# Ten of twelve modulation vectors computed inside the attention stage of a two-layer diffusion backbone

## The chip, the cores and the metric

One core of a Trainium2 chip runs one launch of the kernel. The metric is device time in microseconds (us) of that launch. Engines: TensorE (PE), VectorE (DVE), ScalarE (ACT), GpSimd (POOL) and SyncE (SP, which only issues transfers). Everything is float32. Large products are made as three products of a high and a low float32r part; small ones (scores, transposes, values) as plain float32 products.

## The reference, cut to what matters

Two groups of tokens, 128 context and 512 latent ones of width 1024, go through two layers with shared weights. Each layer has six modulation vectors for each group, from the group's condition vector:

```python
mod_ctx = (jax.nn.silu(c_ctx) @ w_mod[l] + b_mod[l])[None, None, :]
mod_lat = (jax.nn.silu(c) @ w_mod[l] + b_mod[l])[:, None, :]
shift1, scale1, gate1, shift2, scale2, gate2 = jnp.split(mod, 6, axis=-1)
h = rms_norm(x, lp["g_norm1"]) * (1 + scale1) + shift1
mixed, ctx_t = token_mixing(h, lp, lam_init, ctx)     # four attention mixers, gates, w_out
x = x + gate1 * mixed
h = rms_norm(x, lp["g_norm2"]) * (1 + scale2) + shift2
x = x + gate2 * expert_choice_ffn(h, ...)             # 16 experts, each takes its top tokens
```

`w_mod` is 2 x 1024 x 6144 float32, 50 MB. One vector is a 1024-wide sixth of a layer's row, for both groups. The first product needs only shift1 and scale1 of layer 0; gate1 is needed after its attention, shift2, scale2 and gate2 after that, and the six of layer 1 later still.

## The kernel before, in words

**Modulation (front).** For each of 12 vectors q (`for q in range(L * 6)` on TensorE, ScalarE and VectorE), SyncE (L523) brings 8 chunks of 128x1024 of `w_mod` into a ring of 8 slots of 512 KB. ScalarE copies a chunk to its high part (`split_high`, L1023), VectorE subtracts for the low part (`split_low`, L1329), and TensorE (`mod_rows`, L640 to L643) multiplies with `csT`, the conditions in high and low parts. VectorE adds the bias (`mod_evac`, L1371), TensorE adds the high and low rows with `pair_sum` (`mod_tail`, L652), VectorE copies out, for the two scale vectors as (1 + s) times the norm's gain (`mod_copy`, L1385, L1387), and ScalarE stores to `mod_dram` (`mod_store`, L1048). While vector q is split, the first four chunks of vector q + 1 are too; behind the last vector these are the first four chunks of `w_in`.

**Rows from DRAM.** GpSimd loads each vector, broadcast over 128 partitions, as a scale-and-gain or shift tile (`mod_in`, L1787) just before the stage that uses it. The first ones are loaded once vectors 0 and 1 are stored, beside the rest of the front.

**Dense stretch.** Per layer, norm and transposes, then w_in in pieces (D, Aq, Akv), each of four chunks (two of the eight k rows each), tile after tile of 128 tokens (T = 5 tiles); the last tile frees the four chunks. The ring has 8 slots, the high parts 4. From the next piece on, `HIGH` = 4 chunks are split ahead, always when a chunk is freed.

**Attention.** 80 units (a head and a block of 128 queries) in the order D (units 0 to 19), A (20 to 39), B (40 to 59), C (60 to 79). In step ui TensorE makes `scores(ui)`, `turn(ui - 1)` (transposes of the probabilities) and `values(ui - 2)`, and in the three gaps after them (slots 0, 1, 2) what a table gives: chunks of the remaining dense pieces (`W` Bq, Bkv, C; gates `G`; branch outputs `B`), preparation of the next head (`prep`) and turns of o. The table is made by `plan_steps()`; `plan_uses()` gives every item one of two PSUM banks in turn, and an item that comes in while a tile of four chunks is open gets the other bank. All engines walk the same table. VectorE's order in a step is: in A the combination of two probability maps (L1504), the row maximum (L1583, L1588), slot 0, the copy of the fifth transposed block (L1596), slot 1, the scaling of o (L1608), slot 2. TensorE's `values` wait for that copy.

**GpSimd in attention** works in a fixed order: rotary tiles of A, the bias tables of B (`na_load`, L1843), four rotary tiles of C (`rope_c_tile`, L1774 to L1778), with a reload of a bias table that waits for a row maximum of step 46 after the first, then sums of gated outputs (L1889), and the tokens and gate1 for the residual.

**After attention:** the last gates, w_out (two pieces), residual, second norm, router, and 16 experts streamed through a ring of 16 slots that overlays the attention buffers.

## Time and profile before

| | |
|---|---|
| median of 3 runs | 2993.22 us (2990.93 to 2998.76) |
| profiled execution, its own time | 2989.55 us |
| its span, first to last instruction | 2987.6 us |
| granted TensorE clock, mean | 0.961 |
| TensorE, VectorE, ScalarE, GpSimd busy | 90%, 67%, 53%, 15% |
| front: start to the last evacuation of a vector | about 184 us |
| dense stretch of layer 0 | 206 to 285 us |
| attention steps of layer 0 | 285 to 804 us |
| experts of layer 0, of layer 1 | about 1000 to 1540, 2400 to 2940 us |

The profiled execution is one run, 3.7 us below the median. Busy time of a matmul is modelled and overlaps the next; idle time of an engine counts only where another waits for what it does next.

### The profile page before, as it was taken

How to read it: one execution, taken by the hardware profiler on the slowest of the kernel's cores; microseconds unless marked ns; L12 is line 12 of the kernel's file. 1: busy time of each engine (PE TensorE's matmuls, PEld its weight loads, DVE VectorE, ACT ScalarE, POOL GpSimd, SP SyncE). 2: the span in 40 equal slices, each digit the busy share in tenths (PEclk: the TensorE clock that was granted, in tenths of full speed). 3: DMA queues.
4: the chain of work that ended last, by engine and by line, in shares of the span. 5: the costliest groups of instructions: out<-in, count | busy, mean ns of one | idle time of the engine just before them, and what ended most of it. 6: DMA issues, size and time to landing. Idle time of an engine off the chain costs nothing.

```text
span 2987.6 us, 40730 instructions
## 1 busy us (share of the span) xinstructions
PE 2686.8 (90%) x13616; PEld 1916.9 (64%) x13616; DVE 1987.8 (67%) x3069; ACT 1575.4 (53%) x2278; POOL 462.2 (15%) x335
## 2 busy tenths in 40 slices
PE   6779999999996699999988999999999499999994
PEld 1248777777775466666657777777777366666662
DVE  7864356535336799999975346643434699999994
ACT  5643344334323577777753444433422387777773
POOL 0003000212130112112211200031122112211201
PEclk8989999999998899999998999999999699999997
DMA  9942012112144699999983211121134399999994
GB/s 333 333 144 89 29 37 60 50 44 63 67 157 148 231 375 380 381 377 378 381 283 107 73 33 36 36 71 43 43 113 153 113 361 380 382 376 382 381 382 145
DMA packets 190521, 593.80 MB, mean 199 GB/s; under 512 B 22945, under 2 KB 32991, under 8 KB 190391
## 3 DMA queue, kind: packets, MB, share of 16 engines
q1 hardware_dynamic: 171638, 527.66, 48.0%
q0 software_dynamic: 18640, 64.20, 7.4%
q8 instruction: 79, 1.29, 0.2%
q14 instruction: 52, 0.42, 0.0%
q10 hardware_dynamic: 112, 0.23, 0.0%
HBM read 566.78 MB, written 25.23 MB: 198 GB/s over the span
## 4 chain that ended last, share of the span: by engine, by line
PE 77%; DVE 10%; issue 5%; ACT 5%; DMA 2%; ACTq 0%; SPq 0%; POOL 0%; DVEq 0%; POOLq 0%
PE bank L466 21%; PE bank L468 20%; PE bank L467 20%; PE bank L837 4%; PE bank L809 4%; DVE low L1329 2%; ACT high L1023 2%; PE bank L827 2%; PE bank L641 1%; PE bank L640 1%; DMA ring<-in_w_mod 1%; DVE st L1583 1%; PE bank L949 1%; PE bank L981 1%; DVE sigr L1513 1%
## 5 line engine op out<-in xcount | busy, mean ns | idle before, releaser
L1023 ACT ACTIVATE high<-ring 128x1024 fp32r<-128x1024 f32 (+1 forms) x1008 | 1053.8, 1052 | 447.0 <-PE bank L468 369.1
L1736 DVE TENSOR_TENSOR low<-ring,high 128x1024 fp32r<-128x1024 f32 x736 | 880.4, 1220 | 72.7 <-ACT high L1023 70.9
L466 PE MATMUL bank<-high,hT_high 128*128 128x512 f32 (+2 forms) x1280 | 520.9, 407 | 25.2 <-ACT sigr L1109 13.6
L467 PE MATMUL bank<-low,hT_high 128*128 128x512 f32 (+2 forms) x1280 | 485.4, 379 | 0.0
L468 PE MATMUL bank<-high,hT_low 128*128 128x512 f32 (+2 forms) x1280 | 484.2, 378 | 0.0
L1329 DVE TENSOR_TENSOR low<-ring,high 128x1024 fp32r<-128x1024 f32 (+2 forms) x272 | 321.8, 1210 | 138.7 <-ACT high L1023 137.7
L466 PE MATMUL bank<-high,xeT_high 128*80 128x512 f32 x1024 | 406.1, 397 | 2.1 <-DVE xeT_low L1334 2.1
L468 PE MATMUL bank<-high,xeT_low 128*80 128x512 f32 x1024 | 403.9, 394 | 0.0
L467 PE MATMUL bank<-low,xeT_high 128*80 128x512 f32 x1024 | 403.6, 394 | 0.0
L1210 ACT ACTIVATE att<-bank,st 128x640 f32<-128x640 f32 (+3 forms) x200 | 136.7, 684 | 351.2 <-DVE st L1588 256.5
L466 PEld LDWEIGHTS bank<-high,hT_high 128*128 128x128 f32 x1280 | 243.7, 190 | 78.4 <-ACT sigr L1109 18.2
L468 PEld LDWEIGHTS bank<-high,hT_low 128*128 128x128 f32 x1280 | 242.7, 190 | 47.4
L467 PEld LDWEIGHTS bank<-low,hT_high 128*128 128x128 f32 x1280 | 244.3, 191 | 32.5
L1583 DVE TENSOR_REDUCE st<-bank 128x1 f32<-128x640 f32 (+3 forms) x200 | 136.6, 683 | 116.6 <-PE bank L809 114.4
L466 PE MATMUL bank<-high,hidT_high 128*80 128x512 f32 x512 | 203.9, 398 | 10.6 <-DVE hidT_low L1334 8.9
L468 PEld LDWEIGHTS bank<-high,xeT_low 128*80 128x80 f32 x1024 | 151.8, 148 | 84.7 <-issue 0.7
L466 PEld LDWEIGHTS bank<-high,xeT_high 128*80 128x80 f32 x1024 | 151.9, 148 | 83.4 <-DVE xeT_low L1334 2.6
L467 PEld LDWEIGHTS bank<-low,xeT_high 128*80 128x80 f32 x1024 | 152.3, 149 | 80.4 <-issue 0.7
L468 PE MATMUL bank<-high,hidT_low 128*80 128x512 f32 x512 | 202.8, 396 | 0.0
L467 PE MATMUL bank<-low,hidT_high 128*80 128x512 f32 x512 | 202.7, 396 | 0.0
L1923 POOL DMA_INDIRECT x_resid<-oTr,idx_s x32 | 91.5, 2860 | 686.2 <-DVE oTr L1699 667.2
L1914 POOL DMA_INDIRECT U<-x_normed,idx_g x32 | 132.1, 4129 | 327.3 <-issue 104.2
(237 smaller groups left out, 3298.6 us busy)
## 6 DMA issues: line engine op xcount, KB each, us to landing
ring<-in_w_e_gate SPq DMA_DIRECT2D x256, 512.0 KB, 6.2
ring<-in_w_e_up SPq DMA_DIRECT2D x256, 512.0 KB, 6.9
ring<-in_w_e_down SPq DMA_DIRECT2D x256, 512.0 KB, 6.4
ring<-in_w_mod SPq DMA_DIRECT2D x96, 512.0 KB, 6.0
ring<-in_w_gate SPq DMA_DIRECT2D x64, 512.0 KB, 3.9
ring<-in_w_in SPq DMA_DIRECT2D x24, 512.0 KB, 4.5
ring<-in_w_branch SPq DMA_DIRECT2D x16, 512.0 KB, 4.2
ring<-in_w_out SPq DMA_DIRECT2D x16, 512.0 KB, 4.8
```

The lines of the kernel that those rows point to most:

```text
L466: nc.tensor.matmul(out, lhs[0], rhs_high, start=start, stop=False)
L467: nc.tensor.matmul(out, lhs[0], rhs_low, start=False, stop=False)
L468: return nc.tensor.matmul(out, lhs[1], rhs_high, start=False, stop=stop)
L809: ins = mm(ps[p % 2][:, col:col + w], qT[r0:r0 + rn, b, un["m"] * P:(un["m"] + 1) * P], kT[r0:r0 + rn, b, a:a + w], start=True, stop=True)
L837: ins = mm(bank(6, P, P + HD), probT[:, ui % 2, i * P:(i + 1) * P], v_src(un, kb), start=(i == 0), stop=(i == len(un["kb"]) - 1))
L1023: A(high[:, HSLOT[g], :, 0:w], ring[:, SLOT[g], :, 0:w], ACT.Copy).then_inc(high_done, 1)
L1210: A(prob[:, p % 4, 0:w], ps[p % 2][:, 0:w], ACT.Exp, bias=negm[:, p % 8:p % 8 + 1], scale=SCALE[un["br"]], accum_out=sm[:, p % 8:p % 8 + 1 ...
L1329: V.tensor_tensor(low[:, SLOT[g], :, 0:w], ring[:, SLOT[g], :, 0:w], high[:, HSLOT[g], :, 0:w].bitcast(F32), ALU.subtract).then_inc(low_dv ...
L1583: then(V.tensor_reduce(mx[:, c8:c8 + 1], S[:, 0:w], AX.X, ALU.max))
L1736: V.tensor_tensor(low[:, SLOT[ahead], :, :], ring[:, SLOT[ahead], :, :], high[:, HSLOT[ahead], :, :].bitcast(F32), ALU.subtract).then_inc( ...
L1914: pool.indirect_dma_start(out=xe[0:CAP, b, :], out_offset=None, in_=xn_dram, in_offset=bass.IndirectOffsetOnAxis(ap=idx_g[:, b, 0:1], axis ...
L1923: pool.indirect_dma_start(out=x_dram, out_offset=bass.IndirectOffsetOnAxis(ap=idx_s[:, e, 0:1], axis=0), in_=ybuf[0:CAP, e, :], in_offset= ...
```

## The change

Vectors 0 and 1 of layer 0 (shift1, scale1) are still made in the front. The other ten are made in attention: six (gate1, shift2, scale2, gate2 of layer 0, shift1 and scale1 of layer 1) in the attention of layer 0, four (the rest of layer 1) in that of layer 1. A vector is cut into four sums of 256 columns, 24 sums in layer 0 and 16 in layer 1. A sum is made from four pieces; a piece is one transfer of 256 KB (two of the eight k rows, 256 columns) into one of two slots. VectorE multiplies each row by the condition's column of k, for both groups, and accumulates into a tile of 128 x 512 (four instructions of 128x256 a piece). TensorE then adds the 128 partitions by a plain float32 product with a column of ones (128x1), ScalarE copies the 1x512 result to row 0 of the tile, and GpSimd stores it to `raw_dram`. For each four sums GpSimd loads the vector back as 128x16, adds the bias, makes (1 + s) g for the scale vectors, and stores to `mod_dram`. Sum i is added in step 8 + 68 i // 24, slot 1; its pieces stand in the three steps before, in slots 0, 2, 1 and 0. The ring of the dense stages has 6 slots instead of 8; slots 6 and 7 hold the pieces (6) and the accumulators (7).

```diff
 RING_E = 16
 HIGH_E = 8
+RING_D = 6
-N_MOD = 6 * D // NW
-CH_MOD = NQ * N_MOD * L
+CH_MOD = 2 * KD
...
+MOD_COLS = 256
+MOD_ROWS = 2
+VECTORS = [[(0, 2), (0, 3), (0, 4), (0, 5), (1, 0), (1, 1)], [(1, 2), (1, 3), (1, 4), (1, 5)]]
+SUMS = [[(lv, v, a) for lv, v in vs for a in range(D // MOD_COLS)] for vs in VECTORS]
+N_PIECE = KD // MOD_ROWS
+def sum_step(i):
+    return 8 + 68 * i // len(SUMS[0])
...
+    for i in range(len(SUMS[0])):
+        for k in range(N_PIECE):
+            at[sum_step(i) - 3 + 2 * k // 3][2 * k % 3].append(("piece", i, k))
+        at[sum_step(i)][1].append(("sum", i))
...
-        a, h = (SLOT_E[e % RING_E], e % HIGH_E) if e >= 0 else (g % RING, g % HIGH)
+        a, h = (SLOT_E[e % RING_E], e % HIGH_E) if e >= 0 else (g % RING if g < CH_MOD else (g - CH_MOD) % CH_LAYER % RING_D, g % HIGH)
...
+                def mod_fills(step):                      # SyncE
+                    while mods and mods[0][0] < step:
+                        nn = mods.pop(0)[1]
+                        i, k = divmod(nn, N_PIECE)
...
+                        if nn >= 2:
+                            sp.wait_ge(mod_used, MOD_ROWS * (nn - 1))
...
+                        sp.dma_start(mod_w[:, nn % 2, :, :], src).then_inc(mod_w_in[nn % 2], 16)
...
-            for q in range(L * 6):                        # TensorE
+            for q in range(2):
                 mod_rows(q)
                 if q:
                     mod_tail(q - 1)
...
+                def add_partitions(i):
+                    if i < len(SUMS[l]):
+                        n, r = SUM0[l] + i, USE["sum", i]
+                        bank_free(r)
+                        pe.wait_ge(mod_used, KD * (n + 1))
+                        mm(bank_use(r)[0:1, :], ones, mod_acc[:, n % 2, :], start=True, stop=True).then_inc(sum_full, 1)
...
+                def sum_out(i):                           # ScalarE
...
+                        act.wait_ge(sum_full, n + 1)
+                        A(mod_acc[0:1, n % 2, :], bank_use(USE["sum", i])[0:1, :], ACT.Copy).then_inc(sum_ev, 1)
...
+                def mod_piece(i, kp):                     # VectorE
...
+                    dve.wait_ge(mod_w_in[n % 2], 16 * (n // 2 + 1))
+                    if kp == 0 and i >= 2:
+                        dve.wait_ge(raw_out, 16 * (i - 1))
+                    for k in range(MOD_ROWS):
+                        if n or k:
+                            dve.wait_ge(mod_used, MOD_ROWS * n + k)
+                        for g in range(2):
+                            w, cc = mod_w[:, n % 2, k, :], csf[:, MOD_ROWS * kp + k, g:g + 1]
+                            dst = mod_acc[:, i % 2, g * MOD_COLS:(g + 1) * MOD_COLS]
+                            if kp == 0 and k == 0:
+                                ins = V.tensor_scalar(dst, w, cc, None, ALU.mult)
+                            else:
+                                ins = V.scalar_tensor_tensor(out=dst, in0=w, scalar=cc, in1=dst, op0=ALU.mult, op1=ALU.add)
+                        ins.then_inc(mod_used, 1)
...
+            def raw_store(i):                             # GpSimd
+                pool.wait_ge(sum_ev, i + 1)
+                if i:
+                    pool.wait_ge(raw_out, 16 * i)
+                pool.dma_start(raw_dram[...], mod_acc[0:1, i % 2, :]...).then_inc(raw_out, 16)
...
+                mod_work = []
+                for i in range(len(SUMS[l])):
+                    n = SUM0[l] + i
+                    mod_work.append((sum_step(i) + 1.5, raw_store, (n,)))
+                    if i % N_PIECE == N_PIECE - 1:
+                        mod_work.append((sum_step(i) + 2.5, fin_load, (VEC0[l] + i // N_PIECE, n)))
+                        mod_work.append((sum_step(i) + 3.5, fin_store, (VEC0[l] + i // N_PIECE,)))
...
-                rope_c_tile(0)
-                na_reload(0)
-                rope_c_tile(1)
-                rope_c_tile(2)
-                rope_c_tile(3)
+                for m in range(TS):
+                    mod_until(STEP_OF["dense", ("W", "C"), m, NQ - 1])
+                    rope_c_tile(m)
+                    if m == 0:
+                        na_reload(0)
```

`mod_until(step)` makes GpSimd do the parts of `mod_work` that are due before that step; it stands in front of each of its tasks in attention. `fin_load` issues four small loads (six for a scale vector), `fin_store` two or four small GpSimd operations and two stores. GpSimd waits for the vectors before it loads gate1, the rows of the second norm, and those of the next layer.

## Rows read from the trace of the kernel before

**Rows 1.** The page: busy shares; then TensorE, DMA and GB/s in 40 slices.
```profile
PE 2686.8 (90%) x13616; PEld 1916.9 (64%) x13616; DVE 1987.8 (67%) x3069; ACT 1575.4 (53%) x2278; POOL 462.2 (15%) x335
...
PE   6779999999996699999988999999999499999994
...
DMA  9942012112144699999983211121134399999994
```

**Rows 2.** Busy time by stretch: A:B length, PE, PEld, DVE, ACT, POOL, clock, DMA, GB/s.
```profile
50.00:100.00 50.00, 39.32 (x129) 10.17 (x130) 43.38 (x44) 30.78 (x31) 2.09 (x4) 0.90 0.95 349
...
302.00:391.00 89.00, 83.33 (x518) 67.26 (x516) 30.27 (x87) 36.73 (x81) 0.00 (x0) 1.00 0.12 37
391.00:527.00 136.00, 128.37 (x787) 102.70 (x788) 85.30 (x219) 61.02 (x132) 1.12 (x2) 0.99 0.15 45
527.00:660.00 133.00, 125.75 (x710) 101.16 (x709) 67.12 (x151) 47.39 (x89) 28.89 (x27) 1.00 0.16 48
660.00:785.00 125.00, 116.29 (x633) 91.48 (x632) 54.85 (x144) 51.50 (x118) 16.50 (x10) 1.00 0.18 56
```

**Rows 3.** Timeline of SyncE's queue (start, duration): w_mod's first 16 transfers; first small load.
```profile
4.36 25.38 SPq L523 DMA_DIRECT2D ring<-in_w_mod  x16
...
165.01 0.43 SPq L543 DMA_DIRECT2D qn_b<-in_mla_q_norm  x1
```

**Rows 4.** Timeline of VectorE: the last vector's evacuation; the first scaled row of the norm.
```profile
183.59 1.27 DVE L1371 TENSOR_TENSOR U<-bank,U 4x512 f32<-4x512 f32 x2
...
193.21 1.28 DVE L1418 SCALAR_TENSOR_TENSOR att<-att,st,M 128x1024 f32<-128x1024 f32 x1
```

**Rows 5.** Timelines: stores of vector 1 and the last two; broadcast loads; their landing.
```profile
61.14 0.24 ACTq L1048 DMA_DIRECT2D mod_rows<-U  x1
...
186.08 3.97 ACTq L1048 DMA_DIRECT2D mod_rows<-U  x2
...
66.29 0.53 POOL L1787 DMA_DIRECT2D M<-mod_rows  x1 [56.08 <-DMA mod_rows<-U]
...
L1787 POOL DMA_DIRECT2D M<-mod_rows x12: 528/536/601, 66.3 to 2264.3; - x12
...
DMA to landing us min/median/max: 5.0/6.4/10.7
```

**Rows 6.** Timeline of TensorE: two plain float32 products of 512 columns, four records.
```profile
137.25 1.87 PE L652 MATMUL bank<-U,pair_sum 4*2 4x512 f32 x4
```

**Rows 7.** TensorE's waits from 284 to 900: us in total, times, longest.
```profile
PE bank L466 <- ACT sigr L1109: 7.4, 8, 1.4
```

**Rows 8.** VectorE's group of 128x256 (busy, mean ns); two in the timeline.
```profile
L1460 DVE SCALAR_TENSOR_TENSOR sigr<-sigr,st,qn_b 128x256 f32<-128x256 f32 x10 | 4.8, 479 | 0.1
...
236.69 0.48 DVE L1460 SCALAR_TENSOR_TENSOR sigr<-sigr,st,qn_b 128x256 f32<-128x256 f32 x1
237.09 0.34 DVE L1462 SCALAR_TENSOR_TENSOR sigr<-sigr,st,M 128x128 f32<-128x128 f32 x1
```

**Rows 9.** Timelines in a step of D: VectorE's copy; TensorE's values.
```profile
357.02 0.29 DVE L1596 COPY att<-bank 128x128 f32<-128x128 f32 x1
...
357.41 1.30 PE L837 MATMUL bank<-M,att 128*128 128x64 f32 x10 [0.43 <-issue]
```

**Rows 10.** Timeline of GpSimd: reload, rope tiles 1 and 3; landing of L1816's small stores.
```profile
570.77 1.61 POOL L1843 DMA_DIRECT2D att<-rpb_padded  x2 [8.29 <-DVE st L1588]
572.40 1.28 POOL L1774 TENSOR_TENSOR U<-U,rope 128x192 f32<-128x192 f32 x2
...
581.20 2.14 POOL L1774 TENSOR_TENSOR U<-U,rope 128x192 f32<-128x192 f32 x2
...
L1816 POOL DMA_DIRECT2D out<-U x12: 545/565/600, 278.0 to 1972.9; - x12
...
DMA to landing us min/median/max: 1.8/2.5/4.6
```

**Rows 11.** DMA issues by line: transfers of 256 KB, median us to landing.
```profile
ring<-in_w_in SPq DMA_DIRECT2D x16, 256.0 KB, 3.2
```

More of the change, by code:

```diff
@@ L171, in plan_uses @@
     for x in order:
-        if x[0] == "on":
+        if x[0] in ("on", "piece"):
             continue
@@ L184, in plan_uses @@
             open_at = None
+        if x[0] == "sum":
+            freed[r] = ("sum", x[1])
+            continue
         by = "dve" if x[0] == "oT" or (x[0] == "dense" and x[1][0] == "B") else "act"
@@ L205, with mod_step_of @@
 USE, USE_BANK, BEFORE, FREED, FULL, N_USE, LOWS_AFTER, LOWS_END = plan_uses()
+STEP_OF = {x: i for i, step in enumerate(AT) for slot in step for x in slot}
+RELEASE_STEP = [-1] * RING_D + [STEP_OF.get(("dense", pc, T - 1, kq), -1 if pc[0] == "W" else 2 * N_UNIT)
+                                for pc in STREAM for kq in range(CHUNKS_IN[pc])] + [2 * N_UNIT] * (2 * NQ)
+def mod_step_of(n):
+    i, k = divmod(n, N_PIECE)
+    return sum_step(i) - 3 + 2 * k / 3
 def count_of(*key):
@@ L362, in hybrid_step @@
         csf = sb("csf", [P, KD, 2])
+        fin = sb("fin", [P, 3, 16])
+        mod_w = ring[:, RING_D, :, :].rearrange("p h (k n) -> p h k n", k=MOD_ROWS)
+        mod_acc = ring[:, RING_D + 1, :, :]
         csT = sb("csT", [P, KD, 4], F32R)
@@ L375, in hybrid_step @@
         lam, neglam = st[:, 148:150], st[:, 150:151]
+        ones = st[:, 158:159]
         lg = sb("lg", [P, T, NE])
@@ L398, in hybrid_step @@
         g_row_in = sem("g_row_in")
+        ones_set = sem("ones_set")
+        mod_w_in, mod_used = [sem(f"mod_w_in{i}") for i in range(2)], sem("mod_used")
+        sum_full, sum_ev, raw_out = sem("sum_full"), sem("sum_ev"), sem("raw_out")
+        fin_in, fin_out = sem("fin_in"), sem("fin_out")
         eps_set, sq_done = sem("eps_set"), sem("sq_done")
@@ L585, in matrix @@
                             sp.wait_ge(o_ev, N_UNIT * (l + 1))
+                        if i is None and SLOT[g + k] == RING_D:
+                            sp.wait_ge(raw_out, 16 * SUM0[l + 1])
                         if i is None and SLOT[g + k] == 13:
@@ L682, in bank_free @@
                 def bank_free(r):
-                    if BEFORE[r] is not None:
-                        by, n = FREED[BEFORE[r]]
-                        if by == "act":
+                    r = BEFORE[r]
+                    while r is not None and FREED[r][0] == "sum" and FREED[r][1] >= len(SUMS[l]):
+                        r = BEFORE[r]
+                    if r is not None:
+                        by, n = FREED[r]
+                        if by == "sum":
+                            pe.wait_ge(sum_ev, SUM0[l] + n + 1)
+                        elif by == "act":
                             pe.wait_ge(tile_act, N_USE["act"] * l + n)
@@ L857, in between @@
                             dense(*x)
+                        elif what == "sum":
+                            add_partitions(*x)
                         elif what == "prep":
@@ L1053, in _ @@
                 split_high(g)
[L1054 to L1065 removed]
+            bias_in(1)
+            for g in range(HIGH, CH_MOD + HIGH):
+                split_high(g)
+            for q in range(2):
                 mod_store(q)
@@ L1193, in between @@
                             prep_out(*x)
+                        elif what == "sum":
+                            sum_out(*x)
                         elif what == "oT":
                             turn_o_high(*x)
-                        elif x[0] == 2:
+                        elif what == "on" and x[0] == 2:
                             act.wait_ge(on_var, l + 1)
@@ L1357, in _ @@
             V.memset(eps, EPS).then_inc(eps_set, 1)
+            V.memset(ones, 1.0).then_inc(ones_set, 1)
             dve.sem_inc(hid_ready, BUF)
@@ L1391, in _ @@
                 split_low(g)
-            for q in range(L * 6):
+            for q in range(2):
                 for k in range(KD):
@@ L1551, in between @@
                                 split_low(chunk_no(l, c))
+                        elif what == "piece":
+                            mod_piece(*x)
                         elif what == "oT":
@@ L1804, in _ @@
                         mod_in(q1, g)
-                    for b in range(2):
-                        pool.wait_ge(mod_out[b], 16 * 3 * L)
                 def rope_rows(X, t0, tmp, heads, d4):
```

78 lines of the change are left out of this document (62 added, 16 removed).

## The prediction

> **What bounds the kernel now.** I read the page's busy shares and its 40 slices first, then the busy time by stretch, then each engine's timeline and the waits inside a stretch. TensorE is busy 90% of 2987.6 us, VectorE 67%; in the slices two long stretches have TensorE at 9 and DMA at 9 (the experts), and the first slices are different: DMA 9, TensorE 6 to 7 [rows 1]. This is the modulation, bound by streaming 50 MB of w_mod through ring, high/low split and matmul; VectorE is busy 43.4 of 50 us there, TensorE 39.3 [rows 2]. In attention the balance is reversed: TensorE is busy 83.3 of 89, 128.4 of 136, 125.8 of 133 and 116.3 of 125 us in the stretches of mixers D, A, B and C, VectorE 30.3, 85.3, 67.1 and 54.9, and DMA has a share of 0.12 to 0.18 [rows 2]. So DMA has room for anything in attention, VectorE has some, TensorE none: what is added to TensorE counts, and what is added to VectorE counts wherever TensorE waits for it.
>
> **What goes at the front.** SyncE issues its last w_mod transfer at 165.0 (the first small load follows at 165.01), and 18.6 us later, at 183.59, VectorE evacuates the last vector [rows 3, 4]. With two vectors only, the sixteenth w_mod transfer ends its issue at 29.74 [rows 3]; the same 17 small loads and the same four w_in chunks stand between it and the evacuation, so this comes at about 29.8 + 18.6 = 48.4. The shift is 135.2 us, or 13.5 for each of ten vectors.
>
> Part of it is given back. The rows of vectors 0 and 1 must now go through DRAM in the open. Before, the store of vector 1 was issued at 61.14 and GpSimd started the broadcast loads at 66.29, 5.15 later, with nobody waiting; two loads take 2 x 0.53 to issue and 5.0 to 6.4 to land [rows 5]: 11.2 to 12.6 from the store. Before, the last store was issued at 190.05 and the first scaled row started at 193.21 [rows 4, 5], so 8.0 to 9.4 are exposed. The w_in chunks will have landed by then, and GpSimd's small stores land in 1.8 at best and 2.5 in the middle (last line of [rows 10]) rather than 5; against that the slowest of these loads took 10.7. I take 7.5, ends 4 and 12. Net gain of the front: **128**.
>
> **What TensorE gets.** 24 + 16 = 40 products of ones (128x1) with 128x512 plain f32. The nearest row is the product with pair_sum, also f32 and 512 columns: four records in 1.87 us are two products, one record every 0.43, so 0.86 for one [rows 6]. 40 x 0.86 = 34. Some of it will lie under a wait for VectorE in the same step; I take three quarters, 26, ends 15 and 36. ScalarE's 40 copies of 1x512 hide, since it is busy under half of the time in attention [rows 2]; were TensorE not the bound, they would cost some 0.6 each.
>
> A sum also takes one of the two dense banks, and if a tile of four chunks is open in the other, the next tile gets the bank that was just closed and must wait for ScalarE to empty it. That wait exists in attention today behind the preps and the turns of o: 7.4 us in 8 cases [rows 7]. Half of 40 sums at 0.9, a third of them uncovered: 5, ends 0 and 18.
>
> **What VectorE gets.** Each sum has 4 pieces of 4 instructions of 128x256: 160 pieces, 640 instructions. The nearest row is a scalar_tensor_tensor 128x256 of 0.479 us; the next instruction starts 0.40 after it when it doesn't wait [rows 8]. The pair (0.40 + 0.48) is followed by a wait on its own semaphore, some 0.04, so a piece occupies 1.77 and all of them 283 us: 22, 28, 29 and 17 pieces in D, A, B and C of layer 0, 22, 28 and 14 in layer 1. Bounds: fully hidden 0; fully exposed 283.
>
> What is exposed is decided by where a piece stands. In D, VectorE has time, but its copy of the fifth block of transposed probabilities is tied to TensorE: copy at 357.02, done at 357.31, TensorE's values start at 357.41, after an idle of 0.43 [rows 9]. A piece in the first slot of such a step stands between the row maximum and this copy, and TensorE waits for nearly all of it; a piece in the second or third slot falls into an idle of 1 to 2.5 us. About a third of the pieces are of the first kind, at some 1.2: 0.41 each on average, 44 pieces, 18. In A, VectorE's 85 us plus 28 x 1.77 = 50 is 135 of 136 + 6 us: nearly full, in order, and unevenly loaded (splits and gate products come in groups); I take 0.54 for each of 56, 30. In B 0.35 for 43, 15, since the copy there has more slack; in C 0.24 for 17, 4. Together 67, a quarter of 283; for the range 25 and 120. VectorE's fill pushes nothing else that TensorE doesn't already stand for: dense lows are split four chunks ahead.
>
> The Trainium skill (VectorE: DVE Perf Modes, The TRN2 errata) prices a VectorE operation between SBUF tiles at 58 cycles plus one per element: 327 ns for 256 f32 elements, an estimate from that table. The row says 479, and the measurement decides. With 327 the 640 instructions would be 97 us shorter and the sum, at the same exposed quarter, lower by about 25.
>
> **The waits that are new.** VectorE's first piece of sum i waits for the DRAM store of sum i-2, which stands in GpSimd's order. GpSimd runs one rope tile of C, then waits for the maximum of step 46 (its reload starts at 570.77), and ropes tiles 1 and 2 before it comes to the store of sum 13, ahead of tile 3, which starts at 581.20 [rows 10]. VectorE needs that store in the first slot of step 47, one step of 133 / 20 = 6.65 us after that maximum, near 577. With a landing of 2.5 it waits about 7, and behind it stand its maxima and copies. TensorE has some 3 us of other work: 4 per layer, **8**, ends 0 and 16. The weight pieces themselves have two ring slots: 256 KB land in 3.2 us [rows 11], against a lead of 1.3 steps (8 us); only where two sums lie two steps apart is it close, and that is in the 67. SyncE issues them in the order of release, so a late piece holds back only the dense fill behind it. GpSimd's queue gets 40 stores, 46 loads and 20 stores more, at 0.53 each 56 us; it is busy 1.1 of 136 us in A and 28.9 of 133 in B [rows 2], so they hide, except at the place just told.
>
> **The ring shrinks from 8 slots to 6 in the dense stretches.** At D to Aq, Aq to Akv and inside w_out, chunks 3 and 4 of the next piece are fetched only when the last tile before it lets go of its chunks. 3.2 to 4.5 us of landing plus two splits of about 1.1 against four to five chunk times of 0.7 to 1.3: about 1 per border, three per layer, **6**, ends 0 and 20. The expert prefetch starts a little later but has the router's idle stretch to fill 16 slots: nothing.
>
> **Sum:** -128 + 26 + 5 + 67 + 8 + 6 = -16. The profiled execution took 2989.6, so 2974 by its measure; the median of the runs shown is 3.7 above it, hence 2977.
>
> **Rivals.**
> First, attention is elastic: idle time of VectorE in neighbouring steps takes up the pieces, 25 instead of 67 and no wait for stores: -128 + 34 + 25 + 8 = -61, about 2932; anything up to 2955 belongs here. For it: VectorE is at 34 to 63% by stretch [rows 2]. Against: the copy that is already tied to TensorE. Chance 0.24.
>
> Second, on the slow side: a VectorE piece in front of maximum, combine or copy is served in order, and TensorE waits for each. It decides once more than about 0.30 of the 283 us is exposed. At 0.40 it is 113: -128 + 30 + 113 + 19 = +34, about 3027. For it: A would be 95% full and D's copy has 0.1 us of slack. Against: the pieces are spread so that one or two fall in a step of 5 to 7 us. Chance 0.26.
>
> Third, GpSimd's order: its two rope products take 1.28 us in one tile and 2.14 in the next but one [rows 10], and all 38 waits for a store hang on it. At one microsecond each it is 30 more than my 8: about 3007. The Trainium skill (SBUF — State Buffer, SBUF: two separate sides) says that GpSimd and a VectorE operation with two SBUF inputs take a shared port pair in turns, the loser blocked for a whole instruction; the 1.28 and 2.14 would agree with it. Chance 0.07.
>
> Fourth, the change doesn't shorten the front as said, since the tokens or small loads land late when they follow closely: gain 100, about 3005. The tokens were asked for before 10 us, and nothing else is new. Chance 0.05.
>
> My forecast case (2955 to 2995) has 0.38. A measurement of this kernel can tell about 0.3%, 9 us, from no change: faster is below 2984, slower above 3002. The first rival and most of the forecast case give faster 0.51; its upper end and the mild forms of the others give same 0.17; slower 0.32. Range 2938 to 3025.
>
> **What would show it.** Right: first w_in product some 128 us earlier, near 78; about 40 products from mod_acc at 0.86; D, A, B, C of layer 0 longer by about 12, 22, 26 and 8, of layer 1 by as much except C, which stays; experts unchanged. TensorE idle in front of its values, and a VectorE wait of about 7 us on raw_out in step 47 of each layer. Wrong: attention longer by less than 60 (first rival) or by more than 140 (second), or VectorE waits on stores or on mod_w all over. A price of a piece below 1.5 or above 2 would spoil the largest term.

## The result and the profile after

The changed kernel takes **3066.53 us** (median of 4 runs, 3061.86 to 3068.37); the kernel before took 2994.67 in the same comparison (2990.93 to 2998.76). The ratio is 1.0237, 95% interval 1.0218 to 1.0257: slower by 72 us, where I had forecast 16 less and a range that ended at 3025. The profiled execution (its own time, 3068.37, is the highest of the four) has a span of 3066.6 us, 79.0 above that of before.

The front did what was forecast. These are timelines of the kernel after, SyncE's queue first, then VectorE, GpSimd and VectorE again (start, duration, engine, line, operation, output<-inputs, count, idle before and what ended it):

```profile
4.18 26.15 SPq L564 DMA_DIRECT2D ring<-in_w_mod  x16
30.36 0.43 SPq L584 DMA_DIRECT2D qn_b<-in_mla_q_norm  x1
...
48.88 1.27 DVE L1450 TENSOR_TENSOR U<-bank,U 4x512 f32<-4x512 f32 x2
...
57.01 0.53 POOL L1926 DMA_DIRECT2D M<-mod_rows  x1 [46.01 <-DMA mod_rows<-U]
...
62.79 1.28 DVE L1498 SCALAR_TENSOR_TENSOR att<-att,st,M 128x1024 f32<-128x1024 f32 x1 [4.32 <-DMA oTr<-mod_rows]
```

The last evacuation comes at 48.88 instead of 183.59, the first scaled row at 62.79 instead of 193.21 [rows 4]: 130.4 us earlier. So 209 us are lost behind that. To see where, I cut attention at the same instructions in both kernels: VectorE's scaling of o of units 0, 18, 38, 58 and 78, so that the four rows are nearly the mixers D, A, B and C of layer 0. Busy time by stretch (A:B length, PE, PEld, DVE, ACT, POOL, granted clock, DMA share, GB/s), before:

```profile
297.30:391.20 93.90, 87.80 (x551) 71.26 (x551) 32.07 (x93) 38.58 (x85) 0.00 (x0) 1.00 0.11 35
391.20:527.30 136.10, 128.47 (x788) 102.75 (x787) 85.40 (x219) 60.82 (x131) 1.12 (x2) 0.99 0.15 45
527.30:680.50 153.20, 142.98 (x801) 114.75 (x800) 73.05 (x163) 56.18 (x106) 30.05 (x28) 1.00 0.18 56
680.50:798.40 117.90, 111.16 (x601) 87.59 (x600) 59.20 (x150) 45.46 (x107) 23.57 (x15) 1.00 0.16 50
sum 501.10, PE 470.40 PEld 376.36 DVE 249.72 ACT 201.04 POOL 54.74; mean PE 117.60 PEld 94.09 DVE 62.43 ACT 50.26 POOL 13.69
```

and after:

```profile
169.10:279.70 110.60, 98.01 (x573) 74.93 (x572) 68.89 (x186) 42.22 (x90) 6.01 (x12) 0.97 0.27 87
279.70:451.60 171.90, 149.75 (x793) 109.95 (x791) 129.69 (x330) 64.49 (x137) 13.94 (x27) 0.91 0.26 76
451.60:643.20 191.60, 162.62 (x809) 123.05 (x810) 123.21 (x279) 60.10 (x113) 35.02 (x42) 0.92 0.28 85
643.20:781.30 138.10, 123.86 (x611) 91.78 (x610) 87.77 (x213) 48.22 (x112) 35.11 (x39) 0.94 0.23 70
sum 612.20, PE 534.24 PEld 399.70 DVE 409.56 ACT 215.03 POOL 90.08; mean PE 133.56 PEld 99.93 DVE 102.39 ACT 53.76 POOL 22.52
```

Layer 0's attention is 111 us longer: 16.7, 35.8, 38.4 and 20.2 by mixer. The same cut in layer 1, which has 16 sums instead of 24, gives 16.6, 34.6, 28.5 and 1.7 (C has no sum there), 81 in all. Outside attention 17 us more are lost: 2 before the first unit, 7 between attention of layer 0 and of layer 1, 8 behind that of layer 1. 111 + 81 + 17 - 130 = 79, the whole difference of the spans. Attention costs 193 us for 40 sums, 4.8 each, where the prediction's terms for it were 26 + 5 + 67 + 8 = 106.

In these rows VectorE is far from full (409.56 of 612 us) and has 160 us more to do, and two things happen to TensorE. Its idle time, length less busy, goes from 30.7 to 78.0 us. And its busy time grows by 64 us although the 24 products with ones account for some 25: the granted clock falls from 0.99 or 1.00 to between 0.91 and 0.97 while the number of other products stays. One minus the clock, times the length, summed over the four stretches is 42 us after against 1 before; this is an estimate of what the lower clock took. TensorE stalls, and in the same stretches it is also slower in between.

TensorE's and VectorE's waits from 160 to 790 us (engine line waited for: us in total, times, longest) show how short the stalls are:

```profile
PE bank L904 <- issue: 19.7, 11, 5.4
PE bank L507 <- ACT sigr L1178: 11.5, 8, 2.6
PE bank L904 <- ACT att L1301: 9.1, 6, 4.2
PE bank L894 <- DVE att L1584: 4.0, 5, 1.4
...
DVE ring L1612 <- issue: 8.1, 2, 7.0
DVE ring L1614 <- DMA ring<-in_w_mod: 3.2, 2, 2.2
```

L904 is the values, whose input VectorE copies at L1699. The largest of these waits are put down to "issue"; VectorE's timeline in mixer D says what was late:

```profile
194.22 0.82 DVE L1686 TENSOR_REDUCE st<-bank 128x1 f32<-128x640 f32 x1
195.08 0.15 DVE L1691 TENSOR_SCALAR st<-st 128x1 f32<-128x1 f32 x1
195.16 1.80 DVE L1614 SCALAR_TENSOR_TENSOR ring<-ring,csf 128x256 f32<-128x256 f32 x4
197.43 0.62 DVE L1612 TENSOR_SCALAR ring<-ring,csf 128x256 f32<-128x256 f32 x2 [0.47 <-DMA ring<-in_w_mod]
198.08 0.88 DVE L1614 SCALAR_TENSOR_TENSOR ring<-ring,csf 128x256 f32<-128x256 f32 x2
198.88 0.28 DVE L1699 COPY att<-bank 128x128 f32<-128x128 f32 x1
```

and TensorE's, of the same kernel:

```profile
195.06 0.40 PE L509 MATMUL bank<-high,hT_low 128*128 128x512 f32 x1
199.26 2.37 PE L904 MATMUL bank<-M,att 128*128 128x64 f32 x10 [3.81 <-issue]
```

Between the maximum and the copy stand not one piece but two, the last of one sum and the first of the next, with half a microsecond for weights on top; TensorE starts its values 0.10 us after the copy ends, idle for 3.81. In the kernel before, VectorE and TensorE in the same step (the one whose scaling of o is that of unit 5) had

```profile
320.77 0.29 DVE L1596 COPY att<-bank 128x128 f32<-128x128 f32 x1
321.56 1.22 PE L837 MATMUL bank<-M,att 128*128 128x64 f32 x10
```

so the copy was done 0.50 us before TensorE came to its values, which then had no idle time ahead of them. This is one of the worst places: two pieces meet in a slot four times in layer 0 and three times in layer 1, wherever two sums lie two steps apart. Elsewhere a first slot has at most one piece.

VectorE's copies in the four stretches of layer 0, first before, then after (the last numbers: busy, mean ns, idle before), show how its slack went:

```profile
L1596 DVE COPY att<-bank 128x128 f32<-128x128 f32 x46 | 13.4, 290 | 24.8 <-PE bank L827 24.2
L1699 DVE COPY att<-bank 128x128 f32<-128x128 f32 x46 | 13.2, 287 | 6.6 <-PE bank L894 6.1
```

Before, VectorE stood ready ahead of its copies for 24.8 us in all; after, for 6.6, and TensorE's idle time ahead of its values rose from 7.8 to 28.8 us. The copy itself is no slower, nor are the maxima of 640 columns (821 and 820 ns): VectorE's work comes later, it does not take longer.

### The profile page after: what moved, and what is told of

Read it like the earlier page. It is cut to its first block, busy times and chain, and to the rows that moved or that the text cites. A ratio compares the mean times of both kernels' runs of the same rounds, so it can differ in the third digit from the quotient of the medians.

```text
span 3066.6 us, 40985 instructions
## 1 busy us (share of the span) xinstructions
PE 2685.6 (88%) x13336; PEld 1929.1 (63%) x13336; DVE 2135.2 (70%) x3590; ACT 1519.2 (50%) x2238; POOL 500.0 (16%) x457
## 4 chain that ended last, share of the span: by engine, by line
PE 71%; DVE 11%; issue 8%; ACT 5%; DMA 4%; POOL 1%; SPq 0%; ACTq 0%; DVEq 0%; POOLq 0%
PE bank L507 19%; PE bank L509 18%; PE bank L508 18%; PE bank L904 4%; PE bank L876 3%; DVE low L1407 2%; ACT high L1100 2%; PE bank L894 2%; DVE ring L1614 1%; DVE st L1686 1%; PE bank L927 1%; DMA ring<-in_w_in 1%; PE bank L682 1%; PE bank L1058 1%; PE bank L1026 1%
## 5 line engine op out<-in xcount | busy, mean ns | idle before, releaser
L1100 ACT ACTIVATE high<-ring 128x1024 fp32r<-128x1024 f32 (+1 forms) x928 | 973.8, 1052 | 437.1 <-PE bank L509 380.1
L507 PE MATMUL bank<-high,hT_high 128*128 128x512 f32 (+2 forms) x1280 | 529.8, 414 | 43.1 <-ACT sigr L1178 20.3
L508 PE MATMUL bank<-low,hT_high 128*128 128x512 f32 (+2 forms) x1280 | 492.6, 385 | 0.0
L509 PE MATMUL bank<-high,hT_low 128*128 128x512 f32 (+2 forms) x1280 | 491.6, 384 | 0.0
L1288 ACT ACTIVATE att<-bank,st 128x640 f32<-128x640 f32 (+3 forms) x200 | 136.4, 682 | 435.2 <-DVE st L1691 329.9
L1407 DVE TENSOR_TENSOR low<-ring,high 128x1024 fp32r<-128x1024 f32 (+2 forms) x192 | 227.3, 1198 | 129.7 <-ACT high L1100 128.9
L507 PEld LDWEIGHTS bank<-high,hT_high 128*128 128x128 f32 x1280 | 248.0, 194 | 101.1 <-ACT sigr L1178 24.8
L1614 DVE SCALAR_TENSOR_TENSOR ring<-ring,csf 128x256 f32<-128x256 f32 x560 | 254.4, 496 | 9.9 <-DMA ring<-in_w_mod 4.0
```

The source lines that it names most:

```text
L507: nc.tensor.matmul(out, lhs[0], rhs_high, start=start, stop=False)
L508: nc.tensor.matmul(out, lhs[0], rhs_low, start=False, stop=False)
L509: return nc.tensor.matmul(out, lhs[1], rhs_high, start=False, stop=stop)
L1100: A(high[:, HSLOT[g], :, 0:w], ring[:, SLOT[g], :, 0:w], ACT.Copy).then_inc(high_done, 1)
L1288: A(prob[:, p % 4, 0:w], ps[p % 2][:, 0:w], ACT.Exp, bias=negm[:, p % 8:p % 8 + 1], scale=SCALE[un["br"]], accum_out=sm[:, p % 8:p % 8 + 1 ...
L1407: V.tensor_tensor(low[:, SLOT[g], :, 0:w], ring[:, SLOT[g], :, 0:w], high[:, HSLOT[g], :, 0:w].bitcast(F32), ALU.subtract).then_inc(low_dv ...
```

## The experiments

Times are compared by their ratio to the kernel before, timed beside them on the same chip; differences in us are these ratios' differences times 2995. The 95% intervals make a difference of two such ratios good to some 7 to 11 us.

**The ring alone.** The kernel before, with the ring in the dense stretches cut from 8 slots to 6.

```
-  a, h = (SLOT_E[e % RING_E], e % HIGH_E) if e >= 0 else (g % RING, g % HIGH)
+  a, h = (SLOT_E[e % RING_E], e % HIGH_E) if e >= 0 else (g % RING if g < CH_MOD else (g - CH_MOD) % CH_LAYER % RING_D, g % HIGH)
```

> The kernel before with 6 instead of 8 ring slots in the dense stretches, nothing else. My forecast had 6 us for it. In the changed kernel the stretches around attention (first scaled row to first unit, last unit to the experts) are longer by about 9 us per layer. If the ring is the cause of these: 12 to 20 us more than before. If something else there is (vectors read back late, clock): under 6.

Measured: 3008.24 us, ratio 1.0045 (1.0028 to 1.0062), 15 us above the 2993.19 of before, where the prediction had 6. The four stretches of attention kept their lengths (94.1, 136.4, 153.2 and 118.0 in layer 0); the loss is outside, 4 us before the first unit, 6 between the layers' attentions and 5 behind the second. That is most of the 17 us that the kernel after loses there.

**The parts one by one.** The kernel before with 6 slots, and of the change only VectorE's 640 instructions (on data that stay in memory; the first line below), only the 40 products and their copies (the second line), or both. No weights are loaded for them in any of the three, their results are not used, and the front still makes all twelve vectors; slots 6 and 7 are filled once per layer.

```
+  at[sum_step(i) - 3 + 2 * k // 3][2 * k % 3].append(("piece", i, k))
...
+  at[sum_step(i)][1].append(("sum", i))
```

> The kernel before with 6 slots and with VectorE's 640 instructions at the places of the change, on resident data: no w_mod transfer, no product, no store; all twelve vectors still made in the front. Theory A (VectorE serves pieces in order in front of what TensorE waits for; more than half of their 283 us is exposed): 120 to 170 us above the kernel with 6 slots alone, with the granted clock in attention down to 0.9 to 0.95. Theory B (the pieces are mostly hidden, as forecast, and the loss comes from stores, transfers and banks): under 70 above it.

> The kernel before with 6 slots and with the 40 plain products of 128x1 by 128x512 and ScalarE's copies at their places, on resident data; no VectorE work but one clearing per layer. 34 us for the products at 0.86 each, and up to 18 for the order of the two banks: 30 to 50 above the kernel with 6 slots alone. If the bank order were the large term that was missed: 80 or more.

> VectorE's pieces and the products together on resident data, with 6 slots: the change without its transfers, without GpSimd's stores and loads, without the shorter front. Theory A: about 170 to 190 above the kernel with 6 slots alone, so that stores and transfers are left with under 25 of the change's cost. Theory B: under 110. If the two parts hid one another: clearly less than the sum of their single costs.

Measured: 3155.34 (ratio 1.0536, 1.0509 to 1.0563), 3058.03 (1.0211, 1.0191 to 1.0232) and 3183.42 (1.0630, 1.0603 to 1.0657). Above the 3008.24 of the ring alone these are **147**, **50** and **175** us. VectorE's group in the first (layer 0's attention; busy, mean ns, idle before), and TensorE's in the second (48 records, two for each of 24 products):

```profile
L1554 DVE SCALAR_TENSOR_TENSOR ring<-ring,csf 128x256 f32<-128x256 f32 x336 | 155.5, 504 | 3.4
```

```profile
L885 PE MATMUL bank<-ring,ident 128*1 128x512 f32 x48 | 24.5, 591 | 3.3 <-ACT sigr L1144 1.4 <-DVE sigr L1562 1.1 <-ACT U L1136 0.7
```

The price of VectorE's instructions was right (a piece is busy for 1.80 where I had 1.77), and no weight, store or work of GpSimd was added with it: 147 of 283 us, 52%, are exposed with nothing added but this work in VectorE's order. TensorE's clock goes down with it: 0.97, 0.91, 0.92 and 0.95 in the four stretches of layer 0 with VectorE's work alone, against 0.98, 0.99, 1.00 and 1.00 with the products alone. With the products alone TensorE's idle time hardly changes (31.2 us in layer 0's attention for 30.9 with the ring alone). Together the two parts cost 22 less than one by one, as if some of the idle time that VectorE makes covered products. Front -130, ring 15 and both parts 175 make 60; the kernel after shows 72, and the rest, 12, is about the size of what these three kernels leave out, the waits for stores and weights; the waits at step 47, told below, make 10 of it.

**One instruction for four.** The kernel after, but a piece is one 128x512 instruction instead of four of 128x256. The same bytes are loaded, the same places are taken, and the sums are not those of the vectors.

```
-  for k in range(MOD_ROWS):
-      for g in range(2):
-          w, cc = mod_w[:, n % 2, k, :], csf[:, MOD_ROWS * kp + k, g:g + 1]
...
+  for k in range(1):
+      for g in range(1):
+          w, cc = mod_w[:, n % 2, :, :].rearrange("p k n -> p (k n)"), csf[:, MOD_ROWS * kp + k, g:g + 1]
...
```

> The changed kernel with one VectorE instruction of 128x512 a piece in place of four of 128x256 (the sums are then not the vectors' sums; all transfers, waits, products and stores stay). A piece takes about 0.75 instead of 1.8 us. Theory A: the cost of attention falls by 60% of VectorE's part, by 75 to 110 us, so 2955 to 2990. Theory B: stays above 3040.

Measured: 2978.09 us, ratio 0.9935 (0.9915 to 0.9955), 90 us below the kernel after and 19 below that of before. VectorE's groups in layer 0's attention:

```profile
L1614 DVE SCALAR_TENSOR_TENSOR ring<-ring,csf 128x512 f32<-128x512 f32 x72 | 56.5, 785 | 5.6 <-DMA ring<-in_w_mod 4.7 <-issue 0.9
...
L1612 DVE TENSOR_SCALAR ring<-ring,csf 128x512 f32<-128x512 f32 x24 | 11.6, 485 | 11.2 <-DMA mod_raw<-ring 8.2 <-DMA ring<-in_w_mod 2.0 <-issue 0.4
```

The pieces take 68 us here, against 170 in the kernel after. With 60% of VectorE's time gone, 60% of 147, 88, was to be expected if the exposed share is the same for short pieces as for long ones; 90 came back. So the loss goes mostly by VectorE's time, not by the number of places, loads or stores, which are unchanged. TensorE's clock is at 0.95 to 1.00 in the four stretches.

**The place.** No piece in the first slot of a step, that is none between the step's maximum and its copy:

```
+ PIECE_AT = [(-3, 2), (-2, 2), (-1, 1), (-1, 2)]
...
-  at[sum_step(i) - 3 + 2 * k // 3][2 * k % 3].append(("piece", i, k))
+  at[sum_step(i) + PIECE_AT[k][0]][PIECE_AT[k][1]].append(("piece", i, k))
```

> The changed kernel with the pieces in slots 2, 2, 1, 2 of the steps -3, -2, -1, -1 instead of 0, 2, 1, 0: none between the row maximum and the copy of the fifth block. If slot 0 is what costs, as I weighed it in D: 25 to 50 us less than the changed kernel. If any place costs alike, since combination and maximum are delayed instead: within 15 us of it.

Measured: 3057.93, ratio 1.0201 (1.0181 to 1.0221): 11 us better than the kernel after. In D, whose first slot the prediction had named, 5 us are won (105.4 instead of 110.6), in A 3, in B 6 are lost. TensorE's idle time in layer 0 moved rather than went: ahead of the values it fell from 28.8 to 16.2 us, ahead of the dense products it rose from 24.3 to 27.6 and ahead of the sums' products from 4.3 to 13.4. The first slot was not what mattered most; a piece in a later slot is in somebody's way too.

**The grain.** One row of two instructions in each slot in turn instead of a piece of two rows, so that no two rows meet in a slot:

```
+          ROW_AT.append(max(3 * sum_step(_i) - 9 + _k, ROW_AT[-1] + 1 if ROW_AT else 0))
...
-  for k in range(N_PIECE):
-      at[sum_step(i) - 3 + 2 * k // 3][2 * k % 3].append(("piece", i, k))
+  for k in range(KD):
+      at[ROW_AT[KD * i + k] // 3][ROW_AT[KD * i + k] % 3].append(("piece", i, k // MOD_ROWS, k % MOD_ROWS))
```

> The changed kernel with each piece cut in two, one row (two instructions, 0.9 us) in each slot in turn. Same VectorE time, same products. If single delays of 1.8 us exceed a slack of about one microsecond in each slot: 40 to 80 us less. If VectorE's total time is the bound: within 15 us.

Measured: 3033.4, ratio 1.0119 (1.0099 to 1.0139), 35 us better than the kernel after, between the two expectations. So about a quarter of VectorE's 147 us hung on how its work was spread. The version changes two things at once, the size of a lump and the share of the work in first slots (from half to a third), so the 35 are not the lumps' alone; the rest stays with one row to a slot.

**No VectorE at all.** TensorE makes the sums from the weights as they land, in plain f32: eight products of 128x2 with 128x256 in the place of one.

```
-  mm(bank_use(r)[0:1, :], ones, mod_acc[:, n % 2, :], start=True, stop=True).then_inc(sum_full, 1)
...
+  for k in range(KD):
+      ins = mm(bank_use(r, 0, MOD_COLS)[0:2, :], csf[:, k, :], mod_w[:, k // MOD_ROWS, k % MOD_ROWS, :],
+               start=(k == 0), stop=(k == KD - 1))
```

> A version meant to beat both: no VectorE work at all. The four pieces of a sum land in slots 6 and 7, and TensorE multiplies them itself in plain float32, the condition's columns (128x2, both groups) by 128x256, eight products a sum of some 0.21 us each, 1.7 a sum, 68 in all in place of 34; ScalarE copies 2x256. Theory A: front -130, products 68, banks and ring 20 to 28: 2950 to 2970. Theory B: stores, transfers and banks still cost, 3030 or more.

Measured: 3032.35 (3024.86 to 3032.81), ratio 1.0108 (1.0091 to 1.0124). Theory B had such a time, but for another reason. Against theory A it is a miss of some 70 us, which the group of the products in layer 0's attention explains (two records for each of 192 products):

```profile
L925 PE MATMUL bank<-ring,csf 128*2 128x256 f32 x384 | 87.5, 381 | 3.7 <-ACT sigr L1178 1.4 <-DVE sigr L1595 1.1 <-ACT U L1170 1.1
```

A product takes 87.5 / 192 = 0.46 us and a sum 3.6; the four stretches of layer 0 are 109.9, 164.4, 181.6 and 140.9, 95.7 more than before, 4.0 a sum. TensorE has next to no idle time there to hide them in: what goes into its order is paid whole, and a sum at 4.0 costs more than the 3.3 that the front gains for it (130 us for 40).

**GpSimd in VectorE's place**, in layer 1. A row is here a multiplication and an addition for each of the two vectors.

```
-  if i >= len(SUMS[l]):
+  if i >= len(SUMS[l]) or l in GP_LAYERS:
...
+  then(G.tensor_scalar(mod_tmp[:, :], w, cc[:, 0:1], None, ALU.mult))
+  G.tensor_tensor(dst[0], dst[0], mod_tmp[:, :], ALU.add)
+  then(G.tensor_scalar(w, w, cc[:, 1:2], None, ALU.mult))
+  G.tensor_tensor(dst[1], dst[1], w, ALU.add).then_inc(mod_used, 1)
```

> The kernel after, but in layer 1 GpSimd forms the 16 sums in VectorE's place (a product of a weight row with its vector entry, then an addition, for each row and each of the two vectors: 32 instructions of 128x256 a sum instead of 16); layer 0 stays with VectorE. Theory A (VectorE's extra time in its order is what is exposed, and TensorE's product and bank are the rest): layer 1's attention falls from 582 us to what it was with products alone, 523 us, so the kernel to 3066 - 59, about 3007. GpSimd's additions of 128x384 took 1.01 us, so an estimate is 0.7 us an instruction and 26 us a sum, under the 33 us between two sums. Theory B (VectorE and GpSimd disturb each other at the memory, or GpSimd is too slow for its place): VectorE's scans, copies and combines get longer while GpSimd works and TensorE waits for the sums; the time stays at 3050 to 3090.

Measured: 3206.09, ratio 1.0703 (1.0685 to 1.0720), the slowest of all and above both expectations. GpSimd's groups from 1500 to 2500 us, and TensorE's wait from 1650 to 2400:

```profile
L1977 POOL TENSOR_SCALAR mod_tmp<-ring,csf 128x256 f32<-128x256 f32 x112 | 112.5, 1005 | 30.2 <-DMA ring<-in_w_mod 17.8 <-POOL ring L1980 5.4
...
L1978 POOL TENSOR_TENSOR ring<-ring,mod_tmp 128x256 f32<-128x256 f32 x112 | 86.1, 769 | 9.3
```

```profile
PE bank L929 <- POOL ring L1980: 135.2, 16, 32.1
```

A row is 2 x (1.00 + 0.77) = 3.5 us and a sum 28. The 33 us between two sums, on which the expectation rested, was wrong: in layer 1 of the kernel after, the 16 products with ones start 23 us apart on average (1710.7 to 2056.0), since they end at step 50 and not with the attention. So GpSimd, which has rotations and reloads in its order as well, cannot keep up and sets the pace: the products start 32 us apart here, TensorE waits at each of the 16, 135 us in all, and GpSimd is busy 194.9 of 212 us in A. TensorE's granted clock is 0.76, 0.80 and 0.84 in D, A and B. Theory B, by its second half: GpSimd is too slow for the place. Whether it would pay with a sum spread over more steps, no run shows.

**A small product.** The kernel after with 32 of the product's 512 columns; the other columns of the sums are not made.

```
-  mm(bank_use(r)[0:1, :], ones, mod_acc[:, n % 2, :], start=True, stop=True).then_inc(sum_full, 1)
+  mm(bank_use(r, 0, 32)[0:1, :], ones, mod_acc[:, n % 2, 0:32], start=True, stop=True).then_inc(sum_full, 1)
```

> The kernel after with the product with ones and its copy cut to 32 of 512 columns (the other columns of the sums are not made). Theory A (the product's 0.86 us in TensorE's order is exposed, 40 times): 3066 - 33 = about 3033. Theory B (the stalls of VectorE's order hide the product, TensorE being idle anyhow): 3066 - 10 or less, 3056 to 3066. The run of both parts together, which took 22 us less than their sum, speaks for a value between: 3040.

Measured: 3050.0, ratio 1.0181 (1.0164 to 1.0198), 17 us below the kernel after. Between the theories. From its start to the next product a product takes 0.95 us in the kernel after and 0.15 here, so 32 us left TensorE's order and 17 came back: about half lies under stalls that VectorE makes anyway. It agrees roughly with the 22 us by which the two parts overlap.

**The same in one pass.** As the version without VectorE, but the weights are loaded in the rounded f32 type, which TensorE multiplies in one pass. The low parts of weights and of the vector are left out of these ten vectors. The loads come from GpSimd's queue.

```
-  mm(bank_use(r, 0, MOD_COLS)[0:2, :], csf[:, k, :], mod_w[:, k // MOD_ROWS, k % MOD_ROWS, :],
+  mm(bank_use(r, 0, MOD_COLS)[0:2, :], csT[:, k, 0:2], mod_wr[:, k // MOD_ROWS, k % MOD_ROWS, :],
...
+  pool.dma_start(mod_wr[:, k, :, :], src.bitcast(F32R)).then_inc(mod_w_in[0], 16)
```

> Neither VectorE nor a product with ones: GpSimd's queue loads the modulation weights in the rounded one-pass type (the low parts of weights and vector are left out of the ten vectors), and TensorE forms each sum by 8 products of 128x2 by 128x256. In the version with plain products a 256-column product took 0.47 us, 3.8 us a sum, and attention grew by 4.0 us a sum; a one-pass product of 512 columns took 0.40 us in the trace, so one of 256 about 0.2 us, 1.6 us a sum. Theory A (TensorE is the bound in attention and everything put into its order is exposed whole): 40 x 1.6 = 64, plus 16 for bank and order, plus 15 for the ring, less 130 in front: 2997 - 35 = about 2962. Theory B (GpSimd's own order, now with 160 loads in it, makes loads late, each a wait of TensorE): 2990 to 3040.

Measured: **2940.3** (2938.53 to 2943.89), ratio 0.9814 (0.9798 to 0.9831), 22 below what theory A had. The group of the products, in layer 0's attention, and TensorE's waits over the whole span:

```profile
L926 PE MATMUL bank<-low,csT 128*2 128x256 f32 x192 | 27.3, 286 | 9.9 <-DMA low<-in_w_mod 7.3 <-ACT sigr L1179 1.4 <-DVE sigr L1596 1.1
```

```profile
PE bank L926 <- DMA low<-in_w_mod: 13.9, 2, 7.3
```

A product costs 27.3 / 192 = 0.14 us, not the 0.2 that I had taken from the mean of a record, which counts overlapping ends. A sum takes 1.1 us, layer 0's attention 36.5 us more than before, 1.5 a sum, and the clock in its four stretches is 0.97 to 0.99. The Trainium skill (FP8 and Floating Point Precision, TensorE Precision Notes) says that plain f32 takes four passes through the array; 0.46 against 0.14 is a factor of 3.2, so the trace agrees roughly. The Trainium skill also says that a transfer into the rounded type converts and has to be issued by GpSimd (DMA: Bandwidth & Descriptors, SWDGE vs HWDGE vs iDMA); no run here shows it.

**Loads ahead of the reload.** One wait of this version is GpSimd's order, as its timeline shows:

```profile
456.83 1.66 POOL L2013 DMA_DIRECT2D att<-rpb_padded  x2 [8.23 <-DVE st L1694]
...
462.26 2.87 POOL L1973 DMA_DIRECT2D low<-in_w_mod  x4 [0.30 <-POOL U L1884]
```

```
   if m == 0:
+      mod_until(FIRST_UNIT[BLOCKS.index(("B", 0))] + 2 * (TS - 1))
       na_reload(0)
```

> The rounded version (2940), with one edit in GpSimd's order: what is due before step 46, the loads of sum 14 of a layer among it, comes ahead of the reload that waits for that step's maximum. In the rounded version's trace GpSimd waits 8.23 us for this maximum, ropes another tile and issues the four loads at 462.26, and TensorE waits 7.3 us in layer 0 and 6.6 in layer 1 for them. Theory A (in-order GpSimd makes the loads late, and TensorE is bound there): both waits go, 2940 - 12, about 2928, ratio 0.977. Theory B (TensorE falls then into another wait of the same stretch, B, where it idles 18 us): less than 4 us, 2937 to 2941.

Measured: **2923.61** (2911.26 to 2927.29), ratio 0.9747 (0.9726 to 0.9768). In the timeline of this version the loads are issued 16 us earlier:

```profile
446.00 2.92 POOL L1973 DMA_DIRECT2D low<-in_w_mod  x4 [0.30 <-POOL U L1884]
...
453.68 1.63 POOL L2013 DMA_DIRECT2D att<-rpb_padded  x2 [4.23 <-DVE st L1694]
```

TensorE's wait for these loads is gone in both layers, and B is 7.9 and 9.0 us shorter (163.2 and 158.9). The profiled execution gained 11.2 us, as theory A had it; between the ratios of the two versions lie 20, of which I can place no more than the 11. This version beats both kernels: by its median 71 us below the 2994.51 of before, timed beside it, with the same ten vectors made during attention. Like the version it comes from, it leaves their low parts out.

## Why the prediction was wrong

**The front: right.** Forecast -128, measured -130.4 to the first scaled row: the evacuation at 48.88 for 48.4, and the rows' way through DRAM, of which the broadcast loads are 5.8 us from the first issue to the row that uses them, gave back 4.3 us where I took 7.5.

**The size and the count of the new instructions: right.** A piece was 1.77 and is busy for 1.80; the product was 0.86, and its two records start 0.95 before the next product does. The Trainium skill's price for VectorE's instruction (VectorE: DVE Perf Modes, The TRN2 errata; 327 ns, an estimate from its table) was rightly set aside for the row's 479: in the kernel after the mean is 500 ns.

**The exposed share of VectorE: wrong, and this is the failed step.** The prediction took 67 of 283 us, a quarter, as exposed; with VectorE's work alone added 147 were, 52%. The step reasoned place by place: it counted a piece as harmful in the first slot of D, where the copy of [rows 9] had 0.1 us of slack, and as mostly hidden in the other slots since VectorE idles there for 1 to 2.5 us. Two things were missing. The idle time of VectorE at those places is the time in which it waits for TensorE, before the next link of the same chain (maximum, exp, transposition, copy, values); a piece of 1.8 us that starts in it ends behind the moment when VectorE is called, and the rest of the chain is late by the difference. The version without first slots bears this out, with 11 us only, and so do the copies, ahead of which VectorE's idle time fell from 24.8 to 6.6 us. And the pieces were taken one at a time, with a width of 1.77, though seven times in the two layers two of them meet in a slot, as at 195.16 and 197.43; the version by rows, in which none meet, was 35 us faster. My test for A was the sum of busy times, 135 of 142 us. It allows a fit only if the order does not matter. A grew by 36 us.

**The granted clock: not in the sum.** I priced a stall of TensorE at its length. The rows show more: clock 0.91 to 0.97 in the four stretches against 0.99 to 1.00, 42 us of the 111 in layer 0 by the reckoning above. The stretch in which TensorE is idle for the largest share (D in GpSimd's version, 31%) has the lowest clock, 0.76, and those of the one-pass version, where it is idle 39 us in layer 0 against 31 before, 0.97 to 0.99. The order is not strict: A and B of GpSimd's version have 0.80 at 21% and 0.84 at 28%. No run here holds the stalls and changes the clock, so how much of the exposed share is the clock's remains this estimate.

**Products and banks: under by 19.** 26 + 5 was forecast, 50 measured alone. The cover of a quarter that I took does not exist while VectorE is not late: at 0.95 from start to start the 40 products are 38 of the 50. The banks cost little, for TensorE's idle time in the two attentions grew by under 3 us over that of the ring alone; the other 9 or so are busy time that I can't place. In the kernel after, where VectorE is late, about half of the products is covered.

**The ring: 6 forecast, 15 measured**, inside the ends 0 to 20. The place was right (borders of the dense stretches, nothing in attention), the time per border was not 1 but over 2 us.

**The store at step 47: right in place and in VectorE's wait**, 7.00 us in layer 0 and 6.80 in layer 1; TensorE's part was 5.2 in each where I had 4. VectorE's timeline there, and TensorE's, of the kernel after:

```profile
525.97 0.62 DVE L1612 TENSOR_SCALAR ring<-ring,csf 128x256 f32<-128x256 f32 x2 [7.00 <-issue]
526.62 0.88 DVE L1614 SCALAR_TENSOR_TENSOR ring<-ring,csf 128x256 f32<-128x256 f32 x2
527.42 0.28 DVE L1699 COPY att<-bank 128x128 f32<-128x128 f32 x1
```

```profile
527.80 0.66 PE L904 MATMUL bank<-att 128*128 128x64 f32 x2 [5.22 <-issue]
```

GpSimd issues the store at 521.88, it lands at 525.88, and VectorE starts the first piece at 525.97 after a wait of 7.00 us, does the copy, and TensorE has stood 5.22 us. Besides this place only one piece of layer 0 had a wait put down to "issue", 1.1 us, so the third rival, a store's wait at each of 38 sums, did not happen.

The measured terms make -130 + 15 + 175 = 60 of the 72; of the 12 left, TensorE's idle time at the two steps 47 is 10. The outcome is the second rival, in its own words: a piece in VectorE's order is served in order, decided above 0.30 exposed. It had been priced at 0.40 and 3027; with 147 in place of its 113 its sum gives +68, 3061, near the 3066.53 measured. Its chance, 0.26, rested on A being 95% full and on D's copy; what it lacked was the clock and the slots in which two pieces meet. The first rival, an elastic attention, is refuted by the version with VectorE's work alone, 147 us where it had 25.

## What to carry to other kernels

Idle time of an engine inside a chain of dependent steps is not room: ask how long a block of foreign work is against the slack of the next link. Here about half of the added time reached the kernel's time, with blocks of 0.8 us as with blocks of 1.8. Work moved off a streaming-bound stage has to cost less per unit in its new place than the stream did (3.3 us a sum here): VectorE's 4.8 and plain f32's 4.0 did not, one-pass products at 1.5 did, with the low parts left out. VectorE's busy share of 63% in A before the change says nothing of this; an experiment with the extra instructions on resident data does.

## What the runs showed of the hardware

- Stalls of TensorE came with a lower clock: in layer 0's attention, next to 47 us of added idle time, the granted clock was 0.91 to 0.97 instead of 0.99 to 1.00, and TensorE's busy time for the same products grew by about 39 us. With VectorE's instructions alone added, the clock was as low.
- A multiplication of 128x256 f32 by a per-partition scalar took GpSimd 1.00 us and an addition of the same size 0.77; VectorE's form that does both took 0.50. VectorE's row maxima took 821 ns with GpSimd's stream beside them and without; one operation between SBUF tiles (128x640, L1584 in the kernel after) rose from 885 to 1008.
- VectorE's scalar_tensor_tensor took 500 ns for 256 columns and 785 for 512, f32 between SBUF tiles. That leaves a fixed part of some 200 ns, an estimate from these two means. From start to next start a wide one took 0.66 us and a piece of four narrow ones 1.71, so two wide ones would do the work of four in about 80% of the time, an estimate too.
- One-pass products of 256 columns cost 0.14 us each in a row, plain f32 ones 0.46; a plain f32 product of 512 columns 0.95. The mean of one record (0.29 and 0.38) shows neither; the group's busy time over its products does.
